# Attention of a hybrid decoder step: two heads on two halves of the array's rows, probabilities normalised and then turned, values stationary

## The reference, cut to what matters

```python
s = einsum(q, k) * HEAD_DIM ** -0.5 - slopes * dist      # masked outside 0 <= dist <= 128
m = maximum(max(s), sink)
p = exp(s - m)
p = p / (sum(p) + exp(sink - m))
o = einsum(p, v)
```

## Time and profile before

| | us |
|---|---|
| median of 3 runs | 1288.06 (1285.95 to 1288.15) |
| the profiled execution | 1286.84 |
| its span | 1285.1 |
| PE busy | 1194.0 (93%) |
| DVE busy | 732.4 (57%) |
| ACT busy | 535.4 (42%) |
| POOL busy | 182.6 (14%) |

### The profile page before, as it was taken

One profiled execution on the slowest core, in us unless ns is written; L12 is line 12 of the kernel. 1 busy time (PEld: TensorE's weight loads), 2 busy tenths in 40 slices (PEclk: granted clock), 3 DMA queues, 4 the chain that ended last, 5 costly groups with the idle time before them and its releaser, 6 DMA issues.

```text
span 1285.1 us, 22082 instructions
## 1 busy us (share of the span) xinstructions
PE 1194.0 (93%) x8733; PEld 1119.6 (87%) x8733; DVE 732.4 (57%) x1549; ACT 535.4 (42%) x993; POOL 182.6 (14%) x144
## 2 busy tenths in 40 slices
PE   5799999989999998989998999979999999999996
PEld 4699977867888887978987999869999999999996
DVE  5733466546486667387567554554545636446464
ACT  3423356666554454555443322444232332332324
POOL 1400000000033223033211000032010110110100
PEclk9899989989998998989999999979999999999997
DMA  9777412121322220302321238202322222222202
GB/s 300 210 192 266 157 34 67 33 67 34 116 74 69 69 88 13 108 26 68 101 68 52 66 99 271 69 30 67 99 66 99 67 98 94 72 75 90 67 33 74
DMA packets 121258, 120.46 MB, mean 94 GB/s; under 512 B 19268, under 2 KB 111132, under 8 KB 120869
## 3 DMA queue, kind: packets, MB, share of 16 engines
q1 hardware_dynamic: 121157, 119.06, 29.4%
HBM read 109.22 MB, written 11.80 MB: 94 GB/s over the span
## 4 chain that ended last, share of the span: by engine, by line
PE 51%; DVE 10%; ACT 2%; issue 1%; POOL 0%; DVEq 0%; ACTq 0%; POOLq 0%
PE PS L767 43%; PE PS L726 2%; DVE qt L1456 1%; PE PS L882 1%; DVE wR L1298 1%; DVE kt L1457 1%; PE PS L924 1%; DVE att L1474 1%; PE PS L908 1%; DVE xhat L1266 1%; PE PS L931 1%; PE PS L921 0%; PE PS L684 0%; DVE b L1363 0%; DVE tmp L1282 0%
## 5 line engine op out<-in xcount | busy, mean ns | idle before, releaser
L767 PE MATMUL PS<-hR,wR 128*128 128x288 f32 x3744 | 538.9, 302 | 1.9 <-ACT tmp L1068 1.0
L767 PEld LDWEIGHTS PS<-hR,wR 128*128 128x128 f32 x3744 | 514.4, 192 | 18.2 <-issue 13.2
L767 PE MATMUL PS<-actR,wR 128*128 128x288 f32 x1920 | 260.1, 296 | 1.8 <-DVE actR L1440 1.8
L767 PEld LDWEIGHTS PS<-actR,wR 128*128 128x128 f32 x1920 | 256.9, 189 | 2.9 <-DVE actR L1440 2.0
L1298 DVE TENSOR_TENSOR wR<-raw,wR 128x512 fp32r<-128x512 f32 x256 | 202.8, 792 | 90.9 <-ACT wR L993 83.9
L993 ACT ACTIVATE wR<-raw 128x512 fp32r<-128x512 f32 x256 | 161.8, 632 | 140.6 <-PE PS L767 132.9
L1603 POOL TENSOR_TENSOR D<-b 128x512 f32<-128x512 f32 (+1 forms) x56 | 68.2, 1219 | 515.5 <-PE PS L855 285.5
L1630 POOL TENSOR_TENSOR actR<-tmp,actR 128x576 fp32r<-128x576 f32 x32 | 46.2, 1444 | 304.8 <-DVE actR L1351 304.8
L1351 DVE CAST actR<-tmp 128x576 fp32r<-128x576 f32 x32 | 15.2, 476 | 129.5 <-ACT tmp L1087 129.5
L882 PE MATMUL PS<-qt,kt 128*128 128x64 f32 x448 | 61.2, 282 | 23.6 <-DVE qt L1456 20.3
L882 PEld LDWEIGHTS PS<-qt,kt 128*128 128x128 f32 x448 | 57.5, 199 | 28.4 <-DVE qt L1456 25.1
(11 more groups left out here) (212 smaller groups left out, 1298.8 us busy)
## 6 DMA issues: line engine op xcount, KB each, us to landing
raw<-in_w_in SPq DMA_DIRECT2D x26, 1024.0 KB, 5.2
raw<-in_w_up SPq DMA_DIRECT2D x16, 1024.0 KB, 5.6
raw<-in_w_down SPq DMA_DIRECT2D x16, 1024.0 KB, 4.9
mid<-in_w_ada SPq DMA_DIRECT2D x12, 1024.0 KB, 5.2
ada<-in_w_ada SPq DMA_DIRECT2D x8, 1024.0 KB, 12.0
raw<-in_w_in SPq DMA_DIRECT2D x16, 256.0 KB, 6.1
S<-in_state_hgrn SPq DMA_DIRECT2D x8, 512.0 KB, 4.1
out_hgrn_sample<-S SPq DMA_DIRECT2D x8, 512.0 KB, 5.8
```

The costliest lines, as they stand in the source:

```text
L767: mm = pe.matmul(PS[:, 2 * x.pair + h, 0:HALF], weights(x, w, k, col), rhs[r], start=(k == 0 and n == 0), stop=(k == last and n == 2))
```

## The change

- The slots are reordered: a_scale(s-1), a_score(s), a_max(s), a_value(s-2), a_put(s-2), a_exp(s), a_probs(s-1), a_take(s-1). There is one slot less (42 and `win`), and a_turn is gone with its buffer osb.
- a_scale now multiplies the probabilities in SBUF (128x192, or twice 128x256 or 128x128) and comes ahead of a_probs, which waits for it; a_value's result needs no turn, since the values are the stationary operand and the output comes with features on partitions.
- a_value has 64 columns of values stationary and writes to one half of the partitions of A[3] for even heads, the other for odd ones: 4 matmuls in a prompt step (2 in each fourth), 16 in a sample step (before: 2). V's unused rows and probsT's are set to zero once.
- a_score of a prompt step puts its two heads on the two halves of the rows, with two banks, A[0] and A[1]. For that kT gets a second copy of the keys with the halves exchanged: two more copies by ACT for each k tile, ahead of the one that frees the tile. The q weights come in one transfer, in their natural order.

```diff
 def attention_slots():
-    for s in range(PREP, STEPS + 3):
+    for s in range(PREP, STEPS + 2):
         ev = []
-        if s >= PREP + 3:
-            ev += [("a_turn", s - 3), ("a_put", s - 3)]
-        if PREP + 2 <= s < STEPS + 2:
-            ev += [("a_value", s - 2), ("a_scale", s - 2)]
+        if PREP + 1 <= s < STEPS + 1:
+            ev += [("a_scale", s - 1)]
+        if s < STEPS:
+            ev += [("a_score", s), ("a_max", s)]
+        if s >= PREP + 2:
+            ev += [("a_value", s - 2), ("a_put", s - 2)]
+        if s < STEPS:
+            ev += [("a_exp", s)]
         if PREP + 1 <= s < STEPS + 1:
             ev += [("a_probs", s - 1), ("a_take", s - 1)]
-        if s < STEPS:
-            ev = [("a_score", s), ("a_max", s)] + ev + [("a_exp", s)]
         yield ev
...
                 hp, n, g, kts = prompt_step(s)
-                rows = slice((g % 2) * HD, (g % 2 + 1) * HD)
+                k0 = (n - 1 + kts[0]) * P
                 for e in range(2):
-                    j = 2 * (hp % 2) + e
-                    q = qT[rows, (g // 2) * GRP + j, n * P:(n + 1) * P]
-                    k0 = (n - 1 + kts[0]) * P
-                    mm = pe.matmul(A[0][:, e * 2 * P + kts[0] * P:(e + 1) * 2 * P], q, kT[rows, g // 2, k0:(n + 1) * P], start=True, stop=True)
+
+                    rows = slice(e * HD, (e + 1) * HD)
+                    k = kT[rows, g // 2 + (0 if g % 2 == e else 2), k0:(n + 1) * P]
+                    mm = pe.matmul(A[e][:, kts[0] * P:2 * P], qT[rows, hp, n * P:(n + 1) * P], k, start=True, stop=True)
                 mm.then_inc(s_score, 1)
 
             def a_probs(s):
-                pe.wait_ge(s_exp, s - PREP + 1)
+                pe.wait_ge(s_pn, s - PREP + 1)
...
             def a_value(s):
+
                 pe.wait_ge(s_ptc, s - PREP + 1)
...
+                    b = s - PREP
+                    for g in range(KV):
+                        feats = slice(g * HD, (g + 1) * HD)
+                        for old in (True, False):
+                            v = Vc[:, b, feats] if old else V[:, TT, feats]
+                            at = (0 if old else P) + g * GRP * NT
+                            heads = probsT[:, at:at + GRP * NT].rearrange("p (u e t) -> p u e t", e=2, t=NT)
+                            for e in range(2):
+                                mm = pe.matmul(A[3][e * HD:(e + 1) * HD, 2 * g * NT:2 * (g + 1) * NT], v, heads[:, :, e, :], start=old, stop=not old)
                 else:
-                    mm = pe.transpose(A[3][:, 0:P], osb[:, 0:P], ident[:])
-                mm.then_inc(s_ot, 1)
+                    hp, n, g, kts = prompt_step(s)
+                    for kt in kts:
+                        for e in range(2):
+                            mm = pe.matmul(A[3][e * HD:(e + 1) * HD, 0:P], V[:, n - 1 + kt, g * HD:(g + 1) * HD],
+                                           probsT[:, (2 * kt + e) * P:(2 * kt + e + 1) * P], start=(kt == kts[0]), stop=(kt == 1))
+                mm.then_inc(s_pv, 1)
...
-                if x.kind in ("k", "q"):
-                    dst = kT[:, x.n, :] if x.kind == "k" else qT[:, 2 * x.i + x.n, :]
-                    done(act.activation(halves(dst), src, ACT.Copy), s_act_free)
+                if x.kind == "k":
+
+                    done(act.activation(halves(kT[HD:P, 2 + x.n, :]), PS[0:HD, 2 * x.pair:2 * x.pair + 2, 0:HALF], ACT.Copy))
+                    done(act.activation(halves(kT[0:HD, 2 + x.n, :]), PS[HD:P, 2 * x.pair:2 * x.pair + 2, 0:HALF], ACT.Copy))
+                    done(act.activation(halves(kT[:, x.n, :]), src, ACT.Copy), s_act_free)
+                elif x.kind == "q":
+                    done(act.activation(halves(qT[:, 2 * x.i + x.n, :]), src, ACT.Copy), s_act_free)
...
             def a_scale(s):
-                m = small[:, s % 4]
+
+                m, p = small[:, s % 4], probs[s % 2]
                 w = 1 if s < SAMP else 2
                 dve.wait_ge(s_exp, s - PREP + 1)
                 done(dve.tensor_tensor(m[:, 4, 0:w], m[:, 3, 0:w], m[:, 2, 0:w], ALU.add))
                 done(dve.reciprocal(m[:, 4, 0:w], m[:, 4, 0:w]))
-                dve.wait_ge(s_pv, s - PREP + 1)
-                if s > PREP:
-                    dve.wait_ge(s_ot, s - PREP)
...
+                    done(dve.tensor_scalar(p[:, 0:P + SMP], p[:, 0:P + SMP], m[:, 4, 0:1], None, ALU.mult), s_pn)
                     return
-                done(dve.tensor_tensor(osb[:].rearrange("p (e d) -> p e d", e=2), A[2][:, 0:P].rearrange("p (e d) -> p e d", e=2),
-                                       m[:, 4, :].unsqueeze(2).to_broadcast([P, 2, HD]), ALU.mult), s_o)
+                k0 = prompt_step(s)[3][0] * P
+                for e in range(2):
+                    t = p[:, e * 2 * P + k0:(e + 1) * 2 * P]
+                    done(dve.tensor_scalar(t, t, m[:, 4, e:e + 1], None, ALU.mult), s_pn if e else None)
```

More of the change, by code:

```diff
@@ L506, in raw_loads @@
         def raw_loads(u):
-            return sum(64 if UNITS[v][0] == "q" else 16 for v in RING if v <= u and SLOT[v] == SLOT[u])
+            return sum(16 for v in RING if v <= u and SLOT[v] == SLOT[u])
         def prompt_step(s):
@@ L529, in load @@
                 dst = raw[SLOT[u]][:].rearrange("p (k c) -> p k c", c=UC)
[L530 to L537, removed]
                 if kind == "dn":
@@ L1107, in a_take @@
                 if s < SAMP:
-                    done(act.activation(probsT[:, 0:P], A[1][:, 0:P], ACT.Copy))
-                    done(act.activation(probsT[0:SMP, P:2 * P], A[1][0:SMP, P:2 * P], ACT.Copy), s_ptc)
+                    done(act.activation(probsT[:, 0:P], A[2][:, 0:P], ACT.Copy))
+                    done(act.activation(probsT[0:SMP, P:2 * P], A[2][0:SMP, P:2 * P], ACT.Copy), s_ptc)
                     return
                 k0 = prompt_step(s)[3][0] * 2 * P
-                done(act.activation(probsT[:, k0:4 * P], A[1][:, k0:4 * P], ACT.Copy), s_ptc)
+                done(act.activation(probsT[:, k0:4 * P], A[2][:, k0:4 * P], ACT.Copy), s_ptc)
             def a_put(s):
-                act.wait_ge(s_ot, s - PREP + 1)
+                act.wait_ge(s_pv, s - PREP + 1)
                 if s == PREP:
@@ L1119, in a_put @@
                     b = s - PREP
-                    src = A[3][0:HD, 0:P].rearrange("p (k e t) -> p k e t", e=2, t=NT)
                     cols = slice(SEQ + b * NT, SEQ + (b + 1) * NT)
-                    done(act.activation(attnT[0:HD, :, cols], src[:, :, 0, :], ACT.Copy))
-                    done(act.activation(attnT[HD:P, :, cols], src[:, :, 1, :], ACT.Copy), s_otc)
+                    done(act.activation(attnT[:, :, cols], A[3][:, 0:SMP].rearrange("p (k t) -> p k t", t=NT), ACT.Copy), s_otc)
                     return
@@ L1368, in q_blocks @@
                     done(dve.memset(Qblk[:].rearrange("p a b c -> p (a b c)"), 0.0))
+                    done(dve.memset(probsT[SMP:P, P:2 * P], 0.0))
+                    done(dve.memset(V[SMP:P, TT, :], 0.0))
                 dve.wait_ge(s_act_free, count_read(LAST[UNITS.index(("q", i))], "act"))
[L1370 to L1375, removed]
+                rows, T = slice((i % 2) * HD, (i % 2 + 1) * HD), i // 2
+                for j in range(GRP):
+                    c = (i * GRP + j) * NT
+                    src = per_seq(qT[(j % 2) * HD:(j % 2 + 1) * HD, 2 * i + j // 2, SEQ:TOK])
+                    done(dve.tensor_copy(Qblk[rows, T, :, c:c + NT], src), s_qb)
             def a_max(s):
```

37 lines of the change are left out of this document (9 added, 28 removed).

## The result

The changed kernel takes 1333.86 us (median of 4 runs, 1331.54 to 1334.29) against 1287.01 before (4 runs, 1285.41 to 1288.15): a ratio of 1.0361, 95% interval 1.0343 to 1.0380. I had forecast 1337 and a range of 1315 to 1366. The profiled execution has a span of 1329.8, 44.7 more than before.

The account below looks back on a forecast made before the run. PE was taken as the bound in unsplit slots, an ACT-DVE loop in split ones; after, the loop throughout prompt slots. 29.2 + 8.0 + 2.3 + 10 = 49.5 on 1286.8 gave 1337 us, range 1315 to 1366.

Parts of the forecast that it names:

- The loop in split slots: Prompt slots with a split chunk: DVE and ACT waiting on each other take 6.13 us around, 73.6 for 12 slots.
- a sign of being wrong: Listed beforehand as showing the forecast wrong: split prompt slots taking under 5 us.
- The loop in unsplit slots: Prompt slots with an unsplit chunk: scaling, maximum and exponentials take 4.12 us around, mean 4.15, 74.7 for 18 slots.
- evacuations: Between tiles in the prompt stretch: three rq tiles about 2.2 us each, two rf tiles about 3.7 each, 14.0 together.
- PE's savings: Prompt slots: overlapping scores, no turn and cheaper value matmuls leave PE 3.2 to 3.9 us, below 4.12, so only idle time.
- The sample slots: Eight sample slots: PE stays the bound at 5.3 us each, 43.0 against 35.0, so +8.0 us.
- the loop of 4.75: Split sample slots: lo, scale, maximum, exp, take, hi and steps sum to 4.75 us, below PE's 5.3.
- The clock: Prompt stretch: PE's idle time brings more low-clock stretches, 6 slots at 1.7 us, +10 us, ends 0 and 31.
- The k tiles: At the k tiles ahead of attention: extra copies delay the v tile, +2.3 us, ends 1.3 and 2.6.
- The ring of waits: Attention slots: the loop of waits through DVE and ACT becomes the bound, prompt stretch 183.5 against 154.3, +29.2 us.

Follow-up runs that it names:

- b1: Kernel before, with only ScalarE's order changed: exponentials of a slot ahead of the previous slot's copy; 1299.5 us, ratio 1.0115.
- e7: Changed kernel, with VectorE making the weights' low part behind the slot instead of ahead of it in attention; 1298.45 us, ratio 1.0102.
- b2: Kernel before, with VectorE making the weights' low part behind the slot instead of ahead of it; 1275.68 us, ratio 0.9916.
- e5: Changed kernel's operations with one stage more (probabilities, copy, value, put a slot later, scaling behind the maximum); 1291.13 us, ratio 1.0060.
- e8: Changed kernel with one stage more, lo behind the slot, exchanged keys copied later from SBUF, and score ahead of probabilities; 1267.41 us, ratio 0.9844.
- e4_fill: Changed kernel, with PE's idle time in prompt slots filled by matmuls whose result nobody reads; 1333.33 us, ratio 1.0368.
- e1: Changed kernel, with the scaling of the previous slot behind the row maximum instead of ahead of it; 1376.81 us, ratio 1.0711.
- e9: e7 with the exchanged keys copied from SBUF after the k tiles are free; 1294.96 us, ratio 1.0072.

## Why the prediction was right, point by point

- **The loop in split slots: right, and shown.** Predicted 6.13; measured 5.93 and 6.31 in the slots shown, on average 6.35 over the 12 by score starts. Single slots spread from 4.5 to 8.0 between score starts, and three of them are under 5, which I had named as a sign of being wrong. But a score start shifts with whatever PE does before it. From row maximum to row maximum on DVE the 12 take 5.65 to 7.20, 77.3 in all for 73.6; the three of 7.20 (before slots 16, 24 and 36) hold the bias, which I had put into unsplit slots only. Four runs test the loop at different places: the copy behind the exponentials alone adds 0.73 a slot to the kernel before (b1), lo behind the slot takes the loop away in both kernels (e7, b2), one stage more takes it away with the operations kept (e5).
- **The loop in unsplit slots: right in kind, short in size.** 74.7 and 14.0 for evacuations were predicted, 95.0 measured by score starts and 92.8 by row maxima. Two terms were mis-sized. The plain step is 4.26 for 4.12, since the scaling pair takes 0.74 for 0.62, and four steps with one bias among them are 17.4 for 16.6. And an rf tile adds 4.9 where I had 3.7: 3.6 ahead of the next maximum (8.83 for 5.25) and 1.3 behind it (4.93 for 3.65), because ScalarE loads a table for the tile and then another for the exponentials, of which I had counted one. An rq tile adds 2.1 (5.74 for 3.65; 2.2 predicted). Around slot 28:

```profile
286.02 1.28 ACT L1061 ACT_TABLE_LOAD   x1
...
292.44 1.28 ACT L1093 ACT_TABLE_LOAD   x1 [4.17 <-DVE small L1398]
```

  The rest of the 95.0 comes from the mark: slot 41 takes 8.1 by score starts, because PE waits 1.92 for the scaling and then does its chunk at the low clock (2.91) ahead of the next score, while the steps around it are 5.74 and 6.07 by row maxima. In e7, whose split slots are cured, the unsplit steps stay nearly as long (91.9).
- **PE's savings: real and worth nothing, as predicted.** The scores overlap (0.70), the turn is gone, and a_value has 0.66 for 1.00. Only when the loops are opened (e8) do they count.
- **The sample slots: the failed term.** "PE stays the bound" at 5.3 a slot is wrong: I gave a small record 0.07, from loads one behind the other, and it takes 1.04 / 32 = 0.033. The 0.2 for entering and leaving the 64-column tiling had no row behind it; the first and the last group take 0.11 together beyond the 0.117 of the others, within the 1.04. The unsplit slots 9 to 11 are 3.3 to 3.9, no longer than before. The +3.0 comes from the first four, split ones (+2.5; 33.9 for all eight in e7) and from slot 8 (+0.9), where an rq evacuation stands in the loop: the loop of 4.75 that I had put below PE's 5.3 was the bound there, at 4.8 from maximum 6 to 7. By the Trainium skill's rule (TensorE: Matmul & The Clock Gate, LDWEIGHTS), columns over 1.2 GHz, two loads one behind the other would still be, as an estimate, 0.053 each; the measurement is below it. In the kernel before one load of 64 columns took 0.134 and two 0.19, so the second added 0.057; here groups of four start 0.117 apart, 0.029 each, half of that. That loads for the two column halves overlap would explain it; no run here isolates that.
- **The clock: seen as predicted, mis-priced.** It fell to 0.81 in the prompt stretch (0.94 before), but e4_fill, at 0.94 again, is no faster; on the loop the low clock cost about 1 us over 30 slots. The 10 us that I gave it were not there; they happened to make up for what other terms lacked. Where it does cost is at the k tiles: 24 matmuls in 5.49 instead of 3.13. In e1, where PE's chunk is in the loop, slots with a low clock take 7.5 instead of 5.7.
- **The k tiles: right place, partly sized.** PE waited 2.15 + 0.79, against 0.80 before, and the longer ada unit adds 0.2: 2.4 for 2.3 predicted. The low clock behind it adds 2.4; the span up to the first score grew by 3.1, and e9 puts the whole at about 3.5.

Measured less predicted, the terms are -5 (samples), -10 (clock), +6 (unsplit slots), +2.6 (split slots) and +1.3 (the rest): they cancel in part. The ring of waits was the right mechanism, but that the sum came out at 49.5 against 44.7 is partly luck.

## What to carry to other kernels

Before an operation is moved ahead on an in-order engine, follow the ring of waits (the loop above): what does it wait for, who is queued behind it, and does that end at the engine it waits for? Sum the ring over all engines; if it is longer than the fullest engine's work per turn, every instruction on it costs its full duration, and savings elsewhere nothing. Open such a ring by one stage more of distance or by moving an unrelated instruction (here the weights' low part) out of it, before trying cheaper operations. And measure such a ring on an engine that lies on it: the starts of another engine, here PE's scores, shift with that engine's own waits and clock.

## What the runs showed of the hardware that I had not expected

- An fp32 matmul of 64 stationary and 16 streaming columns, alternating between the two halves of the output partitions, costs 0.033 us per record, where 64-column loads one behind the other had taken up to 0.095 and 128-column ones 0.122.
- A low granted clock can be nearly free: at 0.81 and at 0.94 over 190 us the same 30 slots took 170.3 and 169.9 us, where a ring of DVE and ACT was the bound. It lowers the worth of the clock as a reading: ask first whether PE's work is on the ring.
- Scaling 128x256 in place in SBUF takes 0.35 us on DVE (a pair with its gap 0.74), against 0.28 by proportion from 128x576.
